# Four places after the expert stage: transposes moved ahead of a normalisation, an output norm in halves, the last norm read from PSUM, and the L2 norms taken by column sums beside a softmax ring of four

## The reference, cut to what matters

```python
h = rmsnorm_2(x, pre_norm_w)
proj = h @ w_in                       # q_a k_a v_a z_a q_b k_b v_b z_b beta decay gate_a gate_b
o_a = moba_attention(rope(q_a), rope(k_a), v_a)      # 256 tokens: plain causal softmax attention, 8 heads of 128
y_a = (o_a * silu(z_a)) @ w_branch_a
qkv = silu(causal_dwconv(concat(q_b, k_b, v_b), conv_w))     # 4 taps, 3 * 1024 channels
q, k = l2norm(q_b) * 128 ** -0.5, l2norm(k_b)        # x * rsqrt(sum(x*x) + eps), per head and token
o_b = gated_deltanet(q, k, v_b, g, beta)             # chunked delta rule
o_b = rmsnorm_2(o_b, gdn_norm_w)                     # per head and token
y_b = (o_b * silu(z_b)) @ w_branch_b
out = (sigmoid(gate_a) * y_a + sigmoid(gate_b) * y_b) @ w_out
return x + rmsnorm_2(out, post_norm_w)
```

## Time and profile before

| | |
|---|---|
| median of 3 runs | 1484.0 us (1480.49 to 1485.86) |
| profiled execution, its own time | 1481.87 us |
| its span in the trace | 1480.1 us |
| PE busy | 1156.4 us (78%) |
| DVE busy | 764.4 us (52%) |
| ACT busy | 489.3 us (33%) |
| ACT_TABLE_LOADs | 105, 1283 ns each |
| convolution stage, first block on DVE to the last | 1043.14 to 1186.99 us |

### The profile page before, as it was taken

How to read it: one execution, slowest core, us unless ns; L and a number is a source line. 1 busy time by engine, 2 the same in 40 slices (tenths; PEclk the granted TensorE clock), 3 DMA queues, 4 the chain that set the end, 5 groups by cost and what they waited for, 6 DMA issues and landing times.

```text
span 1480.1 us, 14829 instructions
## 1 busy us (share of the span) xinstructions
PE 1156.4 (78%) x5496; PEld 665.9 (45%) x5496; DVE 764.4 (52%) x1783; ACT 489.3 (33%) x1276; POOL 362.9 (25%) x285
## 2 busy tenths in 40 slices
PE   5899775868776676666677766679997798899896
PEld 1688544422331232111122211144775587789782
DVE  2312467668859974455444454420667766632112
ACT  1022122553424333344333233311785542211101
POOL 0678201334334443334333344200000000000000
PEclk9898787989899998989999999989999999999998
DMA  9764413779999999999999999815432211214130
GB/s 336 274 254 165 154 70 143 297 299 411 406 414 420 420 412 391 422 422 421 421 396 397 403 399 421 349 60 184 156 114 80 89 59 59 93 50 143 61 111 28
DMA packets 91875, 377.56 MB, mean 255 GB/s; under 512 B 6323, under 2 KB 9564, under 8 KB 58972
## 3 DMA queue, kind: packets, MB, share of 16 engines
q0 software_dynamic: 36864, 268.45, 44.3%
q1 hardware_dynamic: 53152, 103.98, 19.5%
q10 hardware_dynamic: 1788, 4.19, 0.9%
HBM read 375.54 MB, written 1.06 MB: 254 GB/s over the span
## 4 chain that ended last, share of the span: by engine, by line
PE 43%; DMA 22%; DVE 22%; ACT 9%; issue 3%; POOL 1%; SPq 0%; DVEq 0%; POOLq 0%; ACTq 0%
PE ps L87 43%; DMA AR<-in_puv,idx 19%; DVE AR L87 9%; ACT L87 3%; DVE acc L87 3%; DVE RT L87 2%; DMA W<-in_w_mod 2%; DVE tok L87 2%; ACT av L87 2%; ACT acc L87 1%; DVE rowb L87 1%; DVE mixT L87 1%; ACT AR L87 1%; DVE hT L87 1%; ACT rowb L87 1%
## 5 line engine op out<-in xcount | busy, mean ns | idle before, releaser
L87 PE MATMUL ps<-AR,acc 128*64 128x512 f32 x960 | 367.7, 685 | 186.2 <-ACT acc L87 182.9
L87 POOL DMA_INDIRECT AR<-in_puv,idx x256 | 270.9, 1058 | 519.8 <-PE ps L87 398.3
L87 PE MATMUL ps<-hT,W 128*128 128x256 f32 (+2 forms) x1504 | 322.0, 372 | 3.5 <-ACT acc L87 1.9
L87 PEld LDWEIGHTS ps<-hT,W 128*128 128x128 f32 (+1 forms) x1504 | 268.9, 194 | 56.2 <-issue 14.7
L87 PEld LDWEIGHTS ps<-AR,acc 128*64 128x64 f32 x960 | 89.2, 148 | 438.4 <-ACT acc L87 352.6
L87 DVE CUSTOM_DVE_ANT_0 AR<-AR,mixT 128x1024 f32<-128x1024 f32 x128 | 156.7, 1226 | 156.5 <-DMA AR<-in_puv,idx 156.2
L87 DVE CUSTOM_DVE_ANT_0 AR<-AR,tok 128x1024 f32<-128x1024 f32 x128 | 153.4, 1221 | 61.7 <-DMA AR<-in_puv,idx 61.7
L87 ACT ACTIVATE av<-av 128x1 f32<-128x1 f32 x256 | 51.3, 200 | 306.3 <-DVE av L87 305.4
L87 ACT ACT_TABLE_LOAD x105 | 134.7, 1283 | 17.0 <-issue 15.2
L87 PE MATMUL ps<-W,hT 128*128 128x512 f32 (+3 forms) x288 | 95.5, 488 | 0.0
L87 ACT ACTIVATE acc<-fold,av 128x64 f32<-128x64 f32 x240 | 83.5, 348 | 7.9
(11 more groups left out here) (226 smaller groups left out, 1102.1 us busy)
## 6 DMA issues: line engine op xcount, KB each, us to landing
W<-in_w_in SPq DMA_DIRECT2D x25, 2048.0 KB, 7.8
W<-in_w_mod SPq DMA_DIRECT2D x12, 2048.0 KB, 16.1
W<-in_w_out SPq DMA_DIRECT2D x2, 2048.0 KB, 10.4
W<-in_wq SPq DMA_DIRECT2D x2, 2048.0 KB, 12.8
AR<-in_puv,idx POOLq DMA_INDIRECT x256
W<-in_wba SPq DMA_DIRECT2D x2, 2048.0 KB, 7.8
W<-in_wbb SPq DMA_DIRECT2D x2, 2048.0 KB, 7.7
W<-in_wo SPq DMA_DIRECT2D x2, 2048.0 KB, 7.9
```

What stands on the lines that cost most here:

```text
L87: ins = f(*args, **kw)
```

## The change

Five edits. (1) The two turns of tile 0 stand ahead of `x2_steps(1)` and `norm_T((1,))`. (2) P and the turned P lie in rings of four; `m_turn` comes two steps behind the scores and `m_pv` four. (3) The blocks are convolved in the order q0-3, k0-3, q4-7, k4-7, v (the weight plan follows), and each L2 norm is cut into five parts in five consecutive steps, begun at steps 8, 10, 12, 14, 16, 17, 18, 19: squares; column sums by four matmuls with the squares as weights and one column of ones, and a Sqrt of 128x4; reciprocal of 128x4 and the identity times it (128x512); a product with ones that spreads it over all rows of a bank; two multiplications that read the bank. (4) The output norm is done for each half of `ob`, inside `finish_o`, and `zb_step(2)` stands behind the outputs. (5) In the last stage ACT squares each product out of PSUM with an accumulated sum, the norm of tile 0 is queued ahead of the products of tile 1, and DVE reads the products out of PSUM in halves, with a DMA of 256 KB for each.

```diff
-        for _ in x2_steps(1, t_pelast, t_rot["k", 0]):
-            pass
-        t_xb = t_xb2[1]
-        t_, t_tp = norm_T((1,), tok_at, [t_xb], PV[:, V_PRE:V_PRE + 8], None, [])
...
         rope_turn("q", 0)
         rope_turn("k", 0)
+        for _ in x2_steps(1, t_pelast, t_rot["k", 0]):
+            pass
+        t_xb = t_xb2[1]
+        t_, t_tp = norm_T((1,), tok_at, [t_xb], PV[:, V_PRE:V_PRE + 8], None, [])
...
-            if 1 <= s < 17:
-                m_turn(s - 1)
             if 2 <= s < 18:
-                m_pv(s - 2)
-            if s >= L2:
-                l2_square(s - L2)
-            if s >= L2 + 1:
-                l2_step(s - L2 - 1)
+                m_turn(s - 2)
+            if 4 <= s < 20:
+                m_pv(s - 4)
+            for n, f in enumerate((l2_square, l2_sums, l2_diag, l2_spread, l2_scale)):
+                if s - n in L2:
+                    f(L2.index(s - n))
...
+        def l2_sums(h):
+            b = ps.take()
+            for q in range(4):
+                t = PE(mm, b.t[:, q:q + 1], sqv[:, h % 4, q * 128:q * 128 + 128], ones[:, 0:1], start=True, stop=True,
+                       after=b.old + [t_l2[h]])
+            t_l2[h] = A(act, l2r[:, h, :], b.t[:, 0:4], ACT.Sqrt, bias=eps, after=[t])
+            b.free = [t_l2[h]]
+
+        def l2_diag(h):
+            t = V(rec, l2r[:, h, :], l2r[:, h, :], after=[t_l2[h]])
+            t_l2[h] = V(tt_, sqv[:, h % 4, :].rearrange("p (q t) -> p q t", q=4), ident.unsqueeze(1).to_broadcast([P, 4, P]),
+                        l2r[:, h, :].unsqueeze(2).to_broadcast([P, 4, P]), MUL, after=[t])
+
+        def l2_spread(h):
+            b = ps.take()
+            t = PE(mm, b.t[:, :], ones, sqv[:, h % 4, :], start=True, stop=True, after=b.old + [t_l2[h]])
+            sfree[h % 4] = [t]
+            t_l2[h] = b, t
+
+        def l2_scale(h):
+            b, t = t_l2[h]
+            k1 = V(tt_, qk[:, h, 0, :], qk[:, h, 0, :], b.t[:, 0:256], MUL, after=[t])
+            k2 = V(stt, qk[:, h, 1, :], qk[:, h, 1, :], DK, b.t[:, 256:512], MUL, MUL, after=[t])
+            b.free = [k2]
             t_qk[h] = [k1, k2]
...
             t_ob[n] = [e, t]
+            if g4 == 1:
+                q = osq[:, 8 * a:8 * a + 8]
+                e = A(act, q, q, ACT.Sqrt, scale=1.0 / 128, bias=eps, after=[e])
+                e = V(rec, q, q, after=[e])
+                o = ob[:, 8 * a:8 * a + 8, :]
+                t_on.append(V(tt_, o, o, q.unsqueeze(2).to_broadcast([P, 8, P]), MUL, after=[e]))
...
-                e = A(act, ow[:, a, n * 512:n * 512 + 512], b.t[:, :], ACT.Copy, after=[t, t_on])
...
+                sq.append(A(act, ow[:, a, n * 512:n * 512 + 512], b.t[:, :], ACT.Square, accum_out=v, after=[t] + t_on))
...
+            for n in range(2):
+                c = slice(n * 512, n * 512 + 512)
+                o = ow[:, a, c]
+                t = V(stt, o, bs[n].t[:, :], r, R_POST[:, c], MUL, MUL, after=[e, t_rows[1]])
+                bs[n].free = [t]
+                t = V(tt_, o, o, X[:, a, c], ADD, after=[t])
+                ends.append(SP.dma(nc.sync.dma_start, s_out, out[a * P:a * P + P, c], o, after=[t]))
```

More of the change, by code:

```diff
@@ L169, in build @@
         plan.append((w_in2, 8192, 16))
-        for a in range(4096, 7168, 512):
+        for a in (4096, 5120, 4608, 5632, 6144, 6656):
             plan.append((w_in2, a, 512))
@@ L1368, in build @@
         SCL = 128 ** -0.5
-        Pm = R_G1[:, 0:512].rearrange("p (n k) -> p n k", n=2)
-        PTm = PT[:, :, 0:256].rearrange("p n (k t) -> p n k t", k=2)
-        NB = 2
+        NB = 4
+        Pm = R_G1.rearrange("p (n k) -> p n k", n=NB)
+        PTm = PT[:, 0, :].rearrange("p (n k t) -> p n k t", n=NB, k=2)
         munits = [(a, h) for a in range(2) for h in range(8)]
@@ L1438, in build @@
         sfree = [[t_turn["k", 0], t_turn["k", 1]] for _ in range(4)]
-        L2 = 14
+        L2 = (8, 10, 12, 14, 16, 17, 18, 19)
         t_l2 = {}
+        l2r = sb("l2r", [P, 8, 4])
         def l2_square(h):
-            if h >= 8:
-                return
             f = qk[:, h, :, :].rearrange("p r t -> p (r t)")
             t_l2[h] = V(tt_, sqv[:, h % 4, :], f, f, MUL, after=[t_cv[h], t_cv[8 + h]] + sfree[h % 4])
[L1449 to L1452, removed]
+        def l2_sums(h):
             b = ps.take()
[L1454 to L1460, removed]
+            for q in range(4):
[17 more added lines that the diff above has]
+            b.free = [k2]
             t_qk[h] = [k1, k2]
-        for n in range(6):
+        for n in (0, 2, 1, 3, 4, 5):
             conv_block(n, fill)
@@ L1715, in build @@
         sqfree = []
+        t_on = []
         osq = sb("osq", [P, 16])
@@ L1757, in build @@
             t_vn[1, g4] = [r, e]
-        zb_step(2)
         for g4 in range(2):
@@ L1769, in build @@
             finish_o(b, t, 1, g4)
+        zb_step(2)
         zb_step(3)
-        t = A(act, osq[:, :], osq[:, :], ACT.Sqrt, scale=1.0 / 128, bias=eps, after=[t_ob[3][0]])
-        t = V(rec, osq[:, :], osq[:, :], after=[t])
-        t_on = V(tt_, ob[:, :, :], ob[:, :, :], osq[:, :].unsqueeze(2).to_broadcast([P, 16, P]), MUL, after=[t])
         t_obT = []
@@ L1779, in build @@
                 h, a = 2 * h2 + q // 2, q % 2
-                t = PE(tr, b.t[:, q * 128:q * 128 + 128], ob[:, 8 * a + h, :], ident, after=b.old + [t_on])
+                t = PE(tr, b.t[:, q * 128:q * 128 + 128], ob[:, 8 * a + h, :], ident, after=b.old + t_on)
             o = obT[:, 2 * h2:2 * h2 + 2, :].rearrange("p h t -> p (h t)")
@@ L1790, in build @@
         ow = tok2
-        t_o = [[], []]
         wo = [next_w(), next_w()]
+        s_out = dsem("s_out")
+        ends = []
         for a in range(2):
+            bs, sq = [], []
             for n in range(2):
@@ L1797, in build @@
                 t = token(w, 0, 512, mT, a, t_w_, [t_mg[h] for h in (0, 2, 4, 6)], b, 0)
-                e = A(act, ow[:, a, n * 512:n * 512 + 512], b.t[:, :], ACT.Copy, after=[t, t_on])
[L1799 to L1808, removed]
+                v = st[:, 22 + 2 * a + n:23 + 2 * a + n]
+                sq.append(A(act, ow[:, a, n * 512:n * 512 + 512], b.t[:, :], ACT.Square, accum_out=v, after=[t] + t_on))
+                bs.append(b)
+            r = st[:, 18 + a:19 + a]
+            e = V(tt_, r, st[:, 22 + 2 * a:23 + 2 * a], st[:, 23 + 2 * a:24 + 2 * a], ADD, after=sq)
+            e = A(act, r, r, ACT.Sqrt, scale=1.0 / D, bias=eps, after=[e])
+            e = V(rec, r, r, after=[e])
+            for n in range(2):
[5 more added lines that the diff above has]
+                ends.append(SP.dma(nc.sync.dma_start, s_out, out[a * P:a * P + P, c], o, after=[t]))
+        SP.wait(ends[-1])
         queues = (PE, V, A, G, SP)
```

4 lines of the change are left out of this document (2 added, 2 removed).

## The result

The changed kernel takes 1463.1 us (median of 4 runs, 1462.66 to 1463.74), the kernel before 1482.9 us in the same comparison (1480.49 to 1485.86). The ratio is 0.9866, with a 95% interval of 0.9846 to 0.9886: 19.8 us faster, by the medians. The forecast was 1461.0, with 1453 to 1469 as range. The spans of the two profiled executions differ by 18.5 us, 1480.1 against 1461.6.

The account below looks back on a forecast made before the run. It took PE's idle at the expert stage's end, the DVE-ACT loop with wide reciprocals, the output-norm wait and the ACT-DVE tail as bounds. Gains 1.0 + 11.3 + 6.0 + 4.7 = 23.0 us gave 1461.0, range 1453 to 1469.

Parts of the forecast that it names:

- A: End of expert stage: tile 0's 16 transposes move into PE's 8.47 us idle time; gain 1.0 us.
- B: Convolution stage: ring of four and L2 norms without wide reciprocals, block 8 to second `za_step`; gain 11.3 us.
- D: Last stage: ACT and DVE work after PE's end shrinks from 9.04 to 4.3 us; gain 4.7 us.
- C: Output norm: both halves leave the path, PE's 4.92 us wait goes and its transposes run faster; gain 6.0 us.
- takes back half of the gain: Tile 1's projections: started up to 2.1 us earlier, the first may run at half clock, leaving 1.0 us.
- a loss of 1 if it comes up 3 us later: Tile 1's projections: the bad end of the range, should full clock come 3 us later.
- B, steps 8 to 15: Convolution stage: step times of 5.6 to 7.2 us, with PE's work priced from earlier rows; sum 52.7 us.
- B, steps 16 to 22: Convolution stage without Exp: PE is the bound, with column sums at 1.2 us for four; 36.3 us.
- The ring at nothing: Softmax ring of four: costed at zero, as the step's loop isn't PE's, less 0.4 us for two narrow copies.
- Dearer table loads: Rival, steps 9, 11, 13, 15: a table switch first empties ACT, 5 us more if doubled; 1466, chance 0.03.
- Column sums at 1.9 everywhere: Rival, convolution stage: four sums take 1.9 us, and the moved transposes gain nothing; 17 us gain, 1467, chance 0.16.
- The slower case: Rival, convolution stage: narrow sums and waits drop the clock to 1.2 GHz, about 60 us over 15 steps; 1521, chance 0.03.

Follow-up runs that it names:

- e4: Changed kernel with five useless 128x512 products put into PE's wait ahead of the column sums of step 9; 1464.6 us, ratio 0.9877.
- e5: Kernel before with only the softmax ring of four and its distances (turn two, product four steps behind); 1481.2 us, ratio 0.9991.
- e12: Kernel of e8 with the norms begun one step earlier, at steps 9, 12, 15 to 20; 1451.6 us, ratio 0.9784.
- e8: Changed kernel with tile 0's turns back behind norm_T, ring of two, norms begun at steps 10, 13, 16 to 21; 1457.9 us, ratio 0.9815.
- e10: Changed kernel with tile 0's turns back behind norm_T and a ring of two, its norm starts kept; 1461.9 us, ratio 0.9857.
- e2: Changed kernel with the softmax ring of two and its old distances, all else kept; 1462.3 us, ratio 0.9864.
- e3: Changed kernel with the column sums and all norm parts behind them one step later; 1462.7 us, ratio 0.9859.
- e9: Changed kernel with tile 0's turns back behind norm_T, ring of four, norms begun at steps 10, 13, 16 to 21; 1458.9 us, ratio 0.983.

## Why the prediction was nearly right

**The sum.** 23.0 us were forecast and 18.5 came in the trace (19.8 in the medians). A was 2.0 and B 3.6 too high, D 0.7 and C 0.3 too low. C, D and steps 16 to 22 ran as described. What failed, in A and in steps 9, 13 and 15 of B, is one thing: how long PE runs at half clock. That the time came within 2.1 us of 1461.0 is in part luck: A and the steps up to 15 were 8.4 us too favourable, the steps behind them, C and D 3.8 us too dear, and the medians lie 1.3 us further apart than the two traces.

**A.** The step that failed: "takes back half of the gain". The start at 974.9 was right. The late table load cost nothing: it ended at 967.56, before the Sqrt at 967.78. The half clock cost 3.1 us (44.48 against 41.37 for the 96 passes), all that the earlier start gave and 0.8 to 1.0 more. The other end named there, "a loss of 1 if it comes up 3 us later", is what happened: the clock came up at 981, 4 us behind 977.

**B, steps 8 to 15: 52.7 forecast, 58.9 measured.** Steps 8, 10, 11, 12 and 14 were forecast at 5.6, 6.5, 6.3, 7.2 and 7.2 and measured at 5.53, 6.49, 6.28, 7.15 and 7.15. All the error is in 9, 13 and 15: 8.24, 8.20 and 9.84 instead of 6.3, 6.8 and 6.8, 6.4 us together. The wrong step was to price the work of PE in them at full clock everywhere: "`m_pv` 0.6, column sums 1.2, spread 0.94 and `feat` 3.46". The wait for the scaling in steps 13 and 15 was foreseen, and what stood behind it counted, but not that the same products take a third to six tenths more behind a wait (4.91 to 5.85 us against 3.62). In step 15 all from `m_pv` to the end of `feat` took 9.10 us (1130.99 to 1140.09), in step 17, where PE has no wait, 5.66 (1144.42 to 1150.08); in step 13 it took 7.44. That is 3.4 and 1.8 us, enough for the 3.0 and 1.4 that the two steps are over. Step 9 had no wait in the forecast at all: ahead of its column sums PE has worked off everything and waits for squares that come last in DVE's step. That step 9 takes the 6.29 us of the forecast when PE is kept busy is shown by e4.

**B, steps 16 to 22: 36.3 forecast, 34.3 measured.** PE is the bound, as said. The four column sums take 0.81 from their start to the next product (1144.87 to 1145.68 us in the trace), not 1.2: both groups of the earlier trace rows were too dear for this place. That is 1.6 of the 2.0 us by which this stretch was shorter. The stretch behind block 23's `feat` was shorter by 0.8 (14.1 instead of 14.9). The ring at nothing was right for the kernel before (e5).

**C and D.** C was right in size and place; the halves hide under `zb_step` 2 and 3. In D the DMA of half the size landed in 2.0 instead of 2.6 us; the forecast had named that case, with 5.2, and 5.4 came.

**The rivals.** Dearer table loads are refuted: the load starts at 1106.49, 0.01 behind the end of the copy ahead of it, and the small Sqrt 1.30 us behind the start of its load of 1.28. The Trainium skill ("ScalarE: Activation LUTs", What ACT_TABLE_LOAD costs) gives some 1.38 us of drain on top; the trace has no room for it. Column sums at 1.9 everywhere are refuted by the 0.81 of the dense steps; but behind the waits of steps 9 and 15 the same four took 1.84 and 1.71, as the second group of the earlier trace rows, which also stands behind waits, had it. The other half of that case, no gain in A, came true. The slower case named the right mechanism, the granted clock falling to 1.2 GHz, and priced it over 15 steps; it took three steps and 6 us. From step 16 on PE had work without a break and the granted clock was 1.00. Its ground against, that the pauses go, was wrong: they moved to other steps. Two of the prediction's signs of being wrong did show: sums above 1.5 us for four (1.84 and 1.71), and a granted clock below 0.9 (0.86 in steps 8 to 15, though 0.94 over the stage).

**What stays open.** The two profiles with the ring of two and the change's starts show a stage 7 to 9 us shorter than the changed kernel's, but by the ratios the kernels are only 0.3 and 1.2 us faster. Both profiled executions were the fastest of their five, as that of e12 was. What the other executions did in this stage is in no trace. Their mean granted clock was no higher (0.912 to 0.922, against 0.929 and 0.923 in the profiled ones), so a clock that falls in some executions and not in others would fit, but that was not shown. Also not split: how much of e12's gain over the changed kernel is the ring, since the starts (9, 12, 15 to 20) were not run with four.

## What to carry to other kernels

A wait of the engine that feeds a loop has two prices: its own length, which is free as long as another engine bounds the loop, and the half clock behind it, which is not, because the next products sit on the loop. So price PE's work behind each wait at both clocks, and look whether a deeper ring that lets PE run ahead gathers its spare time in one place: in the traces here it did, but the medians with a ring of two were at most 2.2 us better, within their intervals, so that several short waits are better than a long one is not shown. Work that is added to a loop goes where PE is already the bound or has nothing else to do, but must end before the stage does: starting one step earlier was worth 5.9 us in the traces of e8 and e12, 4.6 by the ratios.

## What the runs showed of the hardware that was not expected

- The length of the last wait does not tell what the clock does. A wait of 1.39 us for P was followed by a `feat` of 4.71 us in e8 and 4.18 in e10, and of 3.62 in e12, with the clock at 1.00.
- A wait on the path can cost more than its length: in e8 the wait of 2.47 us and the slower products behind it made 4.1 us; there 8 passes `K,tiny` took 1.76 us instead of 1.14, and the mean granted clock from 1166.6 to 1173.0 was 0.73.
- Executions of the same instructions scatter ahead of the first edit: in the eight profiles with the old order of the turns, the first turn of tile 1 started between 969.3 and 974.7 us. A difference of spans of two executions below 5 us says nothing; the same stretch repeated to 0.00 us (99.29 in e2 and e10).
- The clock can fall without any wait. Ahead of block 0 PE is busy without a break from 971.93 on in the kernel before, at full clock from 977.01, and then runs 32 passes with only 16 columns and the block's `feat`:

```profile
1033.69 3.64 PE L87 MATMUL ps<-W,hT 128*128 128x16 f32 x32
1037.19 5.39 PE L87 MATMUL ps<-hT,W 128*128 128x256 f32 x16
```

The `feat` takes 5.39 us instead of 3.62, at a mean granted clock of 0.67. It did so in 11 of the 14 profiles; in e3 and e4 the clock fell still earlier (6.59 and 6.37), and in e9 it did not fall (3.70). Whether the narrow passes cause it is not shown: the DMA engines are full at the same time (share 1.04 in the window of that `feat`). The narrow column sums among dense work did not do it (granted clock 1.00 from 1140.7 to 1175 in the changed kernel).
